# One tile of each FFN stage streams 512 columns in place of 256

## The reference, cut to what matters

```python
def conv_ffn(h, w_in, conv_w, conv_b, w_out):          # first model, D_FF = 2816
    z = causal_dwconv(h @ w_in, conv_w, conv_b)         # 3 taps over the tokens
    u, g = jnp.split(z, 2, axis=-1)
    return (jax.nn.gelu(g) * u) @ w_out
...
    h = rms_norm_2(x, g_ffn)                            # second model
    a = depthwise_conv(h @ w_ffn_gate, conv_w, conv_b)
    x = x + (jax.nn.gelu(a) * (h @ w_ffn_up)) @ w_ffn_down
```

## Time and profile before

| what | value |
|---|---|
| three executions | 1563.95, 1567.85, 1569.58 us, median 1567.85 |
| the profiled execution's own time | 1564.95 us |
| its span (first instruction to last) | 1563.1 us |
| matmuls, and as many weight loads | 12,768 |
| granted TensorE clock over the span | 0.999 |
| memory read | 256.04 MB, 164 GB/s over the span |

### The profile page before, as it was taken

The page is one execution under the profiler, slowest core; times in us unless marked ns, Lnnn a source line. Parts: engine busy times, 40 slices in busy tenths (PEclk is TensorE's granted clock), DMA queues, the critical chain, the costliest instruction groups (busy, mean ns, idle before and its releaser), DMA issues.

```text
span 1563.1 us, 30142 instructions
## 1 busy us (share of the span) xinstructions
PE 1538.0 (98%) x12768; PEld 1490.7 (95%) x12768; DVE 1145.2 (73%) x1390; ACT 908.3 (58%) x1213; POOL 158.4 (10%) x91
## 2 busy tenths in 40 slices
PE   7999999999999999999999999999999999999998
PEld 7899999999999999899899999999899899999998
DVE  6668877988887787678458876678778647776666
ACT  6566555798565565456465744456645555644444
POOL 0211211000111210000030110010000013011010
PEclk9999999999999999999999999999999999999999
DMA  9345655534456545333244555544532324556552
GB/s 313 130 165 179 206 190 184 175 149 162 165 186 207 173 160 214 136 109 108 90 160 163 193 196 181 185 164 165 184 136 94 119 96 161 186 189 209 174 188 77
DMA packets 38556, 258.67 MB, mean 165 GB/s; under 512 B 4784, under 2 KB 5552, under 8 KB 7984
## 3 DMA queue, kind: packets, MB, share of 16 engines
q1 hardware_dynamic: 38016, 255.27, 47.3%
q10 hardware_dynamic: 432, 1.84, 0.4%
HBM read 256.04 MB, written 1.05 MB: 164 GB/s over the span
## 4 chain that ended last, share of the span: by engine, by line
PE 77%; issue 13%; ACT 4%; DVE 3%; POOL 1%; DMA 0%; POOLq 0%; SPq 0%; ACTq 0%; DVEq 0%
PE bank L1735 23%; PE bank L1737 22%; PE bank L1736 22%; PE bank L2054 3%; PE bank L2002 2%; PE bank L2027 2%; ACT w_hi L502 1%; DVE w_lo L1010 1%; POOL y_lo L1657 1%; PE bank L1944 1%; PE bank L1971 1%; DVE h_lo L1025 0%; ACT sq L660 0%; ACT qk L658 0%; DVE qk L1126 0%
## 5 line engine op out<-in xcount | busy, mean ns | idle before, releaser
L1735 PE MATMUL bank<-h_hi,w_hi 128*128 128x256 f32 x2640 | 751.6, 285 | 12.5 <-DVE h_lo L1025 9.0
L1736 PE MATMUL bank<-h_lo,w_hi 128*128 128x256 f32 x2640 | 741.6, 281 | 0.0
L1737 PE MATMUL bank<-h_hi,w_lo 128*128 128x256 f32 x2640 | 741.4, 281 | 0.0
L1010 DVE TENSOR_TENSOR w_lo<-raw,w_hi 128x2048 fp32r<-128x2048 f32 x237 | 551.8, 2331 | 166.5 <-ACT w_hi L502 165.7
L502 ACT ACTIVATE w_hi<-raw 128x2048 fp32r<-128x2048 f32 x237 | 452.8, 1912 | 229.9 <-PE bank L1737 229.9
L1735 PEld LDWEIGHTS bank<-h_hi,w_hi 128*128 128x128 f32 x2640 | 497.2, 188 | 24.9 <-issue 12.5
L1737 PEld LDWEIGHTS bank<-h_hi,w_lo 128*128 128x128 f32 x2640 | 500.4, 190 | 0.0
L1736 PEld LDWEIGHTS bank<-h_lo,w_hi 128*128 128x128 f32 x2640 | 497.0, 188 | 0.3
L1735 PE MATMUL bank<-y_hi,w_hi 128*128 128x256 f32 x1040 | 294.9, 284 | 5.2 <-POOL y_lo L1657 2.5
L1737 PE MATMUL bank<-y_hi,w_lo 128*128 128x256 f32 x1040 | 291.6, 280 | 0.0
L1736 PE MATMUL bank<-y_lo,w_hi 128*128 128x256 f32 x1040 | 291.5, 280 | 0.0
(11 more groups left out here) (228 smaller groups left out, 1367.4 us busy)
## 6 DMA issues: line engine op xcount, KB each, us to landing
raw<-W SPq DMA_DIRECT2D x237, 1024.0 KB, 4.8
raw<-W SPq DMA_DIRECT2D x4, 512.0 KB, 7.1
wide<-RW ACTq DMA_DIRECT2D x1, 1280.0 KB, 8.8
x<-XT SPq DMA_DIRECT2D x4, 256.0 KB, 6.3
OUT<-x SPq DMA_DIRECT2D x4, 256.0 KB, 2.0
wide<-CON SPq DMA_DIRECT2D x1, 640.0 KB, 8.6
val<-PE_T ACTq DMA_DIRECT2D x2, 256.0 KB, 2.8
vec<-VEC SPq DMA_DIRECT2D x1, 390.0 KB, 4.9
```

The source lines that it names most:

```text
L1010: V.tensor_tensor(w_lo[:, n0 % NW], raw[:, n0 % NRAW], w_hi[:, n0 % NW].bitcast(F32), ALU.subtract)\
L1735: T.matmul(out, w[0], a[0], start=start, stop=False, **kw)
L1736: T.matmul(out, w[0], a[1], start=False, stop=False, **kw)
L1737: return T.matmul(out, w[1], a[0], start=False, stop=stop, **kw)
```

## The change

A new function `wide_tile` takes the place of the first `column_tile` of unit a in one step of each FFN stage: step 4 in `ffn0` and `ffn1`, step 1 in `hf0` and `hf1`. For tiles k = 0 to 6 of h it makes the high-high matmul with two tiles of `h_hi` as its moving operand, tile k and tile 7 (`k:8:7 - k`), 512 columns over the whole bank, and behind it the low-weights matmul of tile k on 256 columns in the lower half. Then come the seven high-weights matmuls with `h_lo`, and tile 7 by `three` as before. So there are 24 matmuls and 24 weight loads as before, in another order, and 7 of them stream 512 columns. What lands in the upper half of the bank is overwritten by the next `column_tile`, which begins there with `start`. Steps 3 and 4 are written out on TensorE in all FFN stages, and its loop runs twice over steps 5 and 6 (then 7 and 8). The other engines' programs stay as they are.

```diff
+            def wide_tile(n, out):
+
+                for k in range(7):
+                    w = cols(n, k * 256, 128)
+                    T.matmul(out[:], w[0], h_hi[:, k:8:7 - k], start=k == 0, stop=False, skip_group_check=True)
+                    T.matmul(out[:, 0:S], w[1], h_hi[:, k], start=False, stop=False, skip_group_check=True)
+                for k in range(7):
+                    T.matmul(out[:, 0:S], cols(n, k * 256, 128)[0], h_lo[:, k], start=False, stop=False, skip_group_check=True)
+                three(out[:, 0:S], cols(n, 7 * 256, 128), (h_hi[:, 7], h_lo[:, 7]), False, True, skip_group_check=True)
+
...
-                        column_tile(a, 0, ba[:, 0:S])
+                        if s0 == (4 if causal else 1):
+                            wide_tile(a, ba)
+                        else:
+                            column_tile(a, 0, ba[:, 0:S])
                         column_tile(a, 1, ba[:, S:2 * S]).then_inc(sems["w_used"], 1)
...
-                for s0 in range(3):
+                for s0 in range(5):
                     step(s0)
-                with pe.Fori(0, LOOPED // 2) as i:
-                    step(3, i)
-                    step(4, i)
+                with pe.Fori(0, LOOPED // 2 - 1) as i:
+                    step(5, i)
+                    step(6, i)
```

## The result

The changed kernel takes 1568.43 us (median of 22 executions, 1567.1 to 1572.93), the kernel before 1566.0 in the same runs (22 executions, 1561.34 to 1570.02). The ratio is 1.002, with a 95% interval of 1.001 to 1.0029: 0.2% slower, within what I called the same. "Close" and "far" are the two paces of the prediction, 115.56 and 118.33 ns from one product's start to the next. The forecast of 1558.5 lay 9.9 us (0.6%) too low and had the wrong sign; its range, 1555.5 to 1570.5, holds the time. What came is the first rival, "the pace isn't moved", at 1569.6.

The account below looks back on a forecast made before the run. TensorE, busy 98%, was taken to bound the kernel through the distance between product starts. From 1564.95 us profiled, hf0 and hf1 together -7.3, ffn0 +0.9, ffn1 -0.1 gave 1558.4, kept as 1558.5; range 1555.5 to 1570.5.

Parts of the forecast that it names:

- the first rival: All four FFN stages: wide tiles only cost their columns, pace not moved, ffn0 loses its close draw; 1569.6 us, chance 0.29.
- The pace: Behind the wide tile in hf0 and hf1: close pace until the next break, 4.28 us saved each; ffn0 stays close.
- The price of a wide product: Seven 512-column products in one tile per FFN stage: 0.117 us extra each, 0.82 us a stage, 3.28 for four.
- The covers: Waits for `y_lo` hide wide-tile time: all 0.82 us in ffn1, 0.20 in each hf stage, where a restart also vanishes.
- Writing out: Steps 3 and 4 unrolled on TensorE: fetching costs nothing, constant waits let restarts at 161.31 and 466.03 come 0.07 us earlier.
- ffn0's draw: ffn0's restart at 161.31: its lucky close pace is lost for 48 products, 0.13 us, until step 4's wide tile.
- the third rival: ffn1's restart at 466.03 also lands close: 2.4 us less 0.3, giving 1556.3; chance of close in all four stages 0.05.

Follow-up runs that it names:

- the kernel with seven wide and two narrow tiles: Against the kernel before: in all four FFN stages a tile with seven 512-column products, then two reordered tiles at 256 columns; 1561.03 us, ratio 0.9985.

## Why the prediction was right in part, and wrong

- **The step that failed is "The pace".** It said that seven wide products lead TensorE into the close pace, because the product behind a wide one starts when the stream ends. The traces show the opposite: in 14 of 15 tiles with seven wide products whose outcome I read, in this and other kernels, the far pace with its place at 11 follows, also where the stage was close before. The half of the argument that can be checked holds: a weight load lasts 0.19 us in these traces and the start behind a wide product comes 0.235 us after it. It does not lead to the close pace. The 4.28 us a hf stage did not come, and ffn0, which was to be close behind its tile, is far (+3.13 against the forecast +0.9).
- **Why I took the wrong way there.** I had the two paces, and that each holds until a break, from the trace. I had no row with `three` directly behind a wide product and took the mean of wide products (116.7 ns a 256 columns) as a sign. It was none: seven wide products lengthen a unit from 5.680 to between 6.457 and 6.490 us, 0.111 to 0.116 each, whatever state they find. I had seen two things in the change, wider columns and another order, and priced the order at nothing without naming it as a term. From place 8 the order with nothing widened goes to close (26 of 26), and with seven widened to 11 (7 of 7).
- **The price of a wide product** was right: 0.117 taken, 0.115 measured. The Trainium skill (TensorE: Matmul & The Clock Gate, Back-to-back issue gap) gives N/2.4 + 2.5 ns for an isolated product, which would make 256 more columns an estimate of 106.7 ns; the trace is 8% above it, and no run here shows the 109.2 ns that it makes for 256 columns.
- **The covers** held: ffn1's 0.82 us went into its wait (1.05 us between starts became 0.39), the hf restarts are gone, and both hf stages cost 0.60 us, forecast 0.62.
- **Writing out** was priced at nothing, and the run that does it alone is no slower (0.9988). The constant waits came as forecast: TensorE goes 0.05 us behind the end of `y_lo` in the changed kernel where the loop took 0.13.
- **ffn0's draw.** I took it as lost, which the trace shows (+2.8). That the profiled execution was an untypically lucky one of its kernel, by 2.9 us, was a guess from the median of three, and half of it held: ffn0's close pace was a draw, but over 22 executions the median is 1566.0, 1.05 us above the profiled one, and ten of them are faster than it. In the point of 1558.5 the wide tile was to win the draw back.
- **ffn1** was forecast far; this execution is close (-2.07), as in the third rival, but from the wide tile on and not from the restart alone. It is the one tile of the 15 that did what the prediction said, and I can't say why. It is the fastest of the 22; fifteen of them lie between 1567.65 and 1568.82.
- **The chances.** The first rival got 0.29 and was priced at 1569.6; all its terms came in the profiled execution, and ffn1's draw took 2 us off again. The reason it gave, that nearly every break in the trace stays far, was a count of rows (some sixty to two); mine was an argument from one row of another place. The count should have weighed more.

What is open: what the places are inside TensorE. The rule from state to state rests on counts, and it isn't shown why a tile that finds 8 keeps it with one or three wide products and not with seven. Nor is it tested that the other restarts choose at random; that they follow the phase in which a wait ends is my guess. The kernel before spreads over 1553.77 to 1569.2 in one session, seven us of it at a granted clock of 0.999 or more (1559.73 to 1567.17 without the fastest execution), while the kernel with seven wide and two narrow tiles has 1559.64 to 1560.44 there. Draws in four stages, worth 2.7, 2.4, 4.3 and 4.3 us, would make such a spread (1566.37 less all four is 1552.7), but only two of that kernel's executions were seen in a trace. And the 1.7 us at the start and 1.5 in ple0 and hy1, of opposite sign, between the two profiled executions stay unexplained.

## What to carry to other kernels

Where an engine is busy 98% of the time, read the distance between starts, not the busy share, and read it in every stage: here the same code ran 2.4% apart with nothing in the clock, the waits or the DMA to tell of it. A pace in one trace may be a draw, so look at the kernel before twice before you build on it. When a change alters two things at once (columns and order), price each by itself, and try a ladder of sizes in the repeated steps of one kernel: it can show in one execution which of the two does it. And time a kernel with the change's side effects alone in the same session: here that pair lies 4.6 us apart, while each of the two is within 0.2% of the kernel before.

## What I had not expected of the hardware

- A stream of pairs of load and product on 256 columns has two stable paces, 115.56 and 118.33 ns, at the same granted clock of 1.00, and holds either over more than a thousand products. In the far one a distance of 121 or 122 ns comes back every 12 products, at one of a few places.
- The order of 24 products changes the place by a rule that held in 63 of 63 readable cases, without a product more or less: from 11 to 8, to close, to 11. Seven products of 512 columns in that order left 11 in 14 of 15 tiles, from 2, 8, 11 and close alike.
- A wide product costs 0.111 to 0.116 us more than a narrow one where seven stand in a tile, and 0.112 to 0.114 for each one more from two to seven.
- The upper tail of the changed kernel goes with a lower granted clock: the changed kernel's three executions at 0.996 take 1570.36 to 1572.93 us, its seven at 1.000 take 1567.80 to 1568.52.
